# Layer 0 by feature tile: the modulation and the first projection of a hybrid denoising step

## The reference, cut to what matters

```python
def modulate(x, cond, g, w_mod, b_mod):
    mod = jax.nn.silu(cond) @ w_mod + b_mod          # (.., 3 * 1024): shift, scale, gate
    shift, scale, gate = jnp.split(mod[:, None, :], 3, axis=-1)
    return rmsnorm(x, g) * (1 + scale) + shift, gate

def project(x, cond, g, w_mod, b_mod, w_in):
    h, gate = modulate(x, cond, g, w_mod, b_mod)
    return split_proj(h @ w_in), gate
```

## Time and profile before

| | us |
|---|---|
| median of three runs | 1212.49 |
| the profiled execution, whole | 1213.18 |
| its span in the trace | 1211.2 |
| TensorE matmul busy | 1161.9 |
| VectorE busy | 612.7 |
| ScalarE busy | 442.5 |
| GpSimd busy | 364.7 |

### The profile page before, as it was taken

One profiled execution on the slowest core, in us unless ns is written; L12 is line 12 of the kernel. 1 busy time (PEld: TensorE's weight loads), 2 busy tenths in 40 slices (PEclk: granted clock), 3 DMA queues, 4 the chain that ended last, 5 costly groups with the idle time before them and its releaser, 6 DMA issues.

```text
span 1211.2 us, 20038 instructions
## 1 busy us (share of the span) xinstructions
PE 1161.9 (96%) x8022; PEld 1094.5 (90%) x8022; DVE 612.7 (51%) x1412; ACT 442.5 (37%) x1003; POOL 364.7 (30%) x284
## 2 busy tenths in 40 slices
PE   2699999999999999999999999999999999999996
PEld 0489989989989999999999999998999999999996
DVE  3567765765664542152385454676334451334256
ACT  3343535455443111152263344544444311124231
POOL 0123230245360221232362323114424212223342
PEclk9899999999999999999999999999999999999998
DMA  8503131232420112225461201132111011222334
GB/s 346 207 24 140 53 116 55 86 122 62 149 75 19 36 35 105 74 88 171 129 195 40 88 23 60 67 107 67 64 56 50 33 39 36 87 92 78 122 105 161
DMA packets 42860, 110.79 MB, mean 91 GB/s; under 512 B 6032, under 2 KB 21520, under 8 KB 41488
## 3 DMA queue, kind: packets, MB, share of 16 engines
q1 hardware_dynamic: 38736, 105.58, 25.6%
q10 hardware_dynamic: 4032, 3.93, 0.9%
HBM read 99.27 MB, written 10.22 MB: 90 GB/s over the span
## 4 chain that ended last, share of the span: by engine, by line
PE 84%; DVE 3%; issue 0%; ACT 0%; DVEq 0%; ACTq 0%
PE psum L986 67%; PE psum L1015 5%; PE psum L998 5%; PE psum L1006 4%; PE psum L1023 1%; PE psum L1032 1%; DVE xy L1281 1%; PE psum L1133 0%; DVE slots L1370 0%; PE psum L1041 0%; DVE slots L1576 0%; DVE slots L1367 0%; DVE prob L1450 0%; DVE slots L1374 0%; PE psum L188 0%
## 5 line engine op out<-in xcount | busy, mean ns | idle before, releaser
L986 PE MATMUL psum<-h_hi,w_hi 128*128 128x384 f32 x1728 | 604.9, 350 | 8.5 <-DVE h_lo L1253 8.4
L986 PE MATMUL psum<-h_hi,w_lo 128*128 128x384 f32 x1728 | 581.1, 336 | 0.0
L986 PE MATMUL psum<-h_lo,w_hi 128*128 128x384 f32 x1728 | 580.1, 336 | 0.0
L302 POOL TENSOR_TENSOR w_lo<-w_raw,w_hi 128x512 fp32r<-128x512 f32 x144 | 202.7, 1427 | 654.8 <-ACT w_hi L296 654.8
L986 PEld LDWEIGHTS psum<-h_hi,w_hi 128*128 128x128 f32 x1728 | 325.8, 189 | 30.5 <-issue 21.0
L986 PEld LDWEIGHTS psum<-h_lo,w_hi 128*128 128x128 f32 x1728 | 326.5, 189 | 0.0
L986 PEld LDWEIGHTS psum<-h_hi,w_lo 128*128 128x128 f32 x1728 | 325.6, 188 | 0.0
L296 ACT CAST w_hi<-w_raw 128x512 fp32r<-128x512 f32 x144 | 81.9, 618 | 173.2 <-PE psum L986 146.6
L875 ACT ACTIVATE prob<-prob,stat 128x512 f32<-128x512 f32 (+2 forms) x144 | 96.4, 671 | 91.5 <-DVE stat L1440 91.3
L1450 DVE TENSOR_SCALAR prob<-prob,stat 128x512 f32<-128x512 f32 (+1 forms) x144 | 83.4, 579 | 6.5
L882 ACT COPY prob<-psum 128x512 f32<-128x512 f32 (+1 forms) x144 | 75.2, 544 | 27.6 <-PE psum L1006 27.1
(11 more groups left out here) (108 smaller groups left out, 988.3 us busy)
## 6 DMA issues: line engine op xcount, KB each, us to landing
w_raw<-in_w_tiles SPq DMA_DIRECT2D x72, 512.0 KB, 3.3
xy<-in_w_mod SPq DMA_DIRECT2D x32, 512.0 KB, 4.3
table<-in_rpb SPq DMA_DIRECT2D x48, 192.0 KB, 3.5
slots<-in_w_mod SPq DMA_DIRECT2D x8, 1024.0 KB, 6.6
table<-in_w_tiles SPq DMA_DIRECT2D x16, 512.0 KB, 3.6
xy<-in_xT SPq DMA_DIRECT2D x8, 576.0 KB, 7.3
slots<-in_xT SPq DMA_DIRECT2D x8, 384.0 KB, 4.8
x_kept<-xy SPq DMA_DIRECT2D x8, 384.0 KB, 5.3
```

The source lines that it names most:

```text
L302: nc.gpsimd.tensor_tensor(w_lo[:, w % 2, a:b], RAW[raw_at(w)][:, a:b], w_hi[:, w % 2, a:b], ALU.subtract).then_inc(s.lo_ready, 1)
L986: last = nc.tensor.matmul(psum[:, bank, 0:CH], a[:, w % 2, k, :], h[:, k, cols], start=(k == order[0] and a is w_hi and h is h_hi), stop=( ...
```

## The change

The first block is gone; its work stands at the head of the second one, and each engine goes on without meeting the others. The modulation weights of layer 0 come in another layout: block k holds the shift and the scale columns of feature tile k for all 1024 inputs (again 1 MB). So each block finishes one feature tile. Tokens are projected feature tile by feature tile: for tile k the chunks 0 and 1 are one piece of 768 columns and chunk 2 (in two parts, latent and context) another, only tile 0 goes in three pieces; both output tiles and all three chunks accumulate at once in the six banks. The row of shifts and scales for tile k + 3 is made between the chunks of tile k.

```diff
@@ sync queue: four constants ahead of x instead of seven, masks last
+            for k in range(KT):
+                sp.dma_start(xy[:, k], xT[k]).then_inc(x_in[k], 16)
+            for k in range(KT):
+                if k >= 3:
+                    sp.wait_ge(wmod_used, k - 2)
+                sp.dma_start(wmod_sb[:, k % 3], w_mod0[k]).then_inc(wmod_in[k % 3], 16)
+                if k < 2:
+                    load_weights(sp, 0, k)
@@ ScalarE
+            def copy_row(k):
+                act.wait_ge(wmod_used, k + 1)
+                if k >= AHEAD:
+                    act.wait_ge(modT_ready, k - AHEAD + 1)
+                nc.scalar.copy(modrow[:, k % AHEAD], psum[:, ROW_BANK, 0:2 * P]).then_inc(modrow_ready, 1)
...
+            for k in range(KT):
+                act.wait_ge(x_in[k], 16)
+                if k > 2:
+                    act.wait_ge(squares_added, k - 2)
+                nc.scalar.activation(square_of(k) if k else squares, xy[:, k], ACT.Square).then_inc(x_squared, 1)
+            high_half(act, 0, 0)
+            copy_row(0)
+            high_half(act, 0, 1)
+            copy_row(1)
+            for c in range(NCH):
+                act.wait_ge(pro_norm[1], 3 * (c + 1))
+                nc.scalar.copy(first_rstd[:, cols_of(c)], psum[:, RSTD_BANK + c, 0:CH]).then_inc(pro_copied, 1)
+            copy_row(2)
+            for k in range(KT):
+                make_high(k)
+                if k + AHEAD < KT:
+                    copy_row(k + AHEAD)
@@ TensorE
+            def make_rows(k):
+                pe.wait_ge(wmod_in[k % 3], 16 * (k // 3 + 1))
+                if k >= 1:
+                    pe.wait_ge(modrow_ready, k)
+                for i in range(2):
+                    for q in range(4):
+                        last = nc.tensor.matmul(psum[32 * q:32 * q + 32, ROW_BANK, 0:2 * P], silu_c[:, 4 * i + q, :],
+                                                wmod_sb[:, k % 3, (4 * i + q) * 2 * P:(4 * i + q + 1) * 2 * P],
+                                                start=(i == 0), stop=(i == 1), skip_group_check=True)
+                last.then_inc(wmod_used, 1)
...
+            make_rows(0)
+            sums(0)
+            turn_row(0)
+            sums(1)
+            sums(2)
+            make_rows(1)
+            turn_row(1)
+            for c in range(NCH):
+                spread(c)
+            make_rows(2)
+            pe.wait_ge(pro_copied, NCH)
+            for k in range(KT):
+                project(k, 0)
+                if k + AHEAD < KT:
+                    make_rows(k + AHEAD)
+                project(k, 1)
+                if k + 2 < KT:
+                    turn_row(k + 2)
+                project(k, 2)
@@ VectorE: per tile the three modulation steps, then scaled and low by piece
+            for k in range(KT):
+                if k > 0:
+                    take_mods(k)
+                last = len(first_parts(k)) - 1
+                for i in range(last + 1):
+                    if k == 0:
+                        dve.wait_ge(pro_copied, i + 1)
+                    make_scaled(k, i)
+                    if i > 0:
+                        make_low(k, i - 1)
+                make_low(k, last)
+            settle()
```

More of the change, by code:

```diff
@@ new lines, in build, with first_parts @@
+        tanh_c = vectors[:, 272:272 + 2 * KT].rearrange("p (k c) -> p k c", c=2)
+        bmod_sb = vectors[:, 288:288 + 24 * DEPTH].rearrange("p (l n) -> p l n", l=DEPTH)
+        square_of = lambda k: slots[:, 10 if k % 2 else 7]
+        first_rstd = slots[:, 6]
+        first_scaled = (slots[:, 9], slots[:, 10])
+        AHEAD = 3
+        HALVES = ([(slice(0, 2 * CH), 0)], pieces(NCH - 1))
+        ROW_BANK, TURN_BANK, SUM_BANK = 6, 7, 0
+        def first_parts(k):
+            return [pieces(c) for c in range(NCH)] if k == 0 else HALVES
@@ new lines, in tensor_start, with turn_row, spread, project @@
+        def tensor_start(pe):
+            s = signals[0]
+            def make_rows(k):
[8 more added lines that the diff above has]
+                last.then_inc(wmod_used, 1)
+            def turn_row(k):
+                pe.wait_ge(modrow_ready, k + 1)
+                if k >= 1:
+                    pe.wait_ge(mod_taken, k)
+                for j in range(2):
+                    last = nc.tensor.transpose(psum[:, TURN_BANK, j * P:(j + 1) * P], modrow[:, k % AHEAD, j * P:(j + 1) * P],
+                                               ident[:, :])
+                last.then_inc(modT_ready, 1)
+            def spread(c):
+                for t in range(3 * c, 3 * c + 3):
+                    pe.wait_ge(pro_norm[0], t + 1)
+                    nc.tensor.matmul(psum[:, RSTD_BANK + c, (t % 3) * P:(t % 3 + 1) * P], ones[:, :], diag[:, t],
+                                     start=True, stop=True).then_inc(pro_norm[1], 1)
+            def project(k, c):
+                if c == 0 and k % 4 == 0:
+                    pe.wait_ge(s.lo_ready, k // 4 + 1)
+                if k == 0 or c != 1:
+                    pe.wait_ge(s.h_lo_ready, first_count(k, c if k == 0 else c // 2))
+                for n in range(2):
+                    if k % 4 == 0 and c == 0 and n == 1:
+                        pe.wait_ge(s.lo_ready, 2 + k // 4 + 1)
+                    for w, h in ((w_hi, h_hi), (w_hi, h_lo), (w_lo, h_hi)):
+                        last = nc.tensor.matmul(psum[:, 3 * n + c, 0:CH], w[:, n, k, :], h[:, k, cols_of(c)],
+                                                start=(k == 0 and w is w_hi and h is h_hi),
+                                                stop=(k == KT - 1 and w is w_lo), skip_group_check=True)
+                    if k == KT - 1:
+                        last.then_inc(s.chunk_done, 1)
+            def sums(c):
+                pe.wait_ge(squares_added, KT - 2 + c + 1)
+                for t in range(3 * c, 3 * c + 3):
+                    nc.tensor.matmul(psum[:, SUM_BANK, t:t + 1], squares[:, t * P:(t + 1) * P], ones[:, 0:1],
+                                     start=True, stop=True).then_inc(pro_sums, 1)
+            pe.wait_ge(cond_ready, 1)
+            pe.wait_ge(pro_ones, 1)
+            pe.wait_ge(consts_in, 16 * CONSTS)
+            make_rows(0)
[17 more added lines that the diff above has]
+                project(k, 2)
@@ L923, in y_high @@
                     nc.scalar.copy(h_hi[:, k, cols_of(c)], xy[:, k, cols_of(c)]).then_inc(s.y_hi_ready, 1)
[L925 to L931 removed]
+            if layer > 0:
                 for k in range(KT):
```

270 lines of the change are left out of this document (119 added, 151 removed).

## The result

The changed kernel takes 1208.85 us (median of six runs, 1205.76 to 1211.32), the kernel before 1213.37 (six runs). The ratio is 0.9967, interval 0.9953 to 0.9981: 4.5 us by the medians, 4.0 by the ratio. The forecast was 7.4. The six runs lie up to 5.6 us apart, the faster ones with the higher mean granted clock (see e8). The profiled execution of the changed kernel has a span of 1206.4 us against 1211.2.

The account below looks back on a forecast made before the run. TensorE is nearly always busy from 81 us, so tile 2's start decides: 32.4 + 6.8 + 4 x 4.95 + 2 x 4.25 + 3.2 = 70.7, with wait and clock 74.2 instead of 81.6; 1205.1 us, range 1199.5 to 1210.5.

Parts of the forecast that it names:

- the ring: Feature loop: projection, row, ScalarE's row copy, then next tile's high and low parts; 4.95 us per step, over TensorE's 4.65.
- the wait for tile 2: Behind the feature loop: TensorE waits about 2.6 us (2.3 to 3.8) for weight tile 2's low half.
- the transfer of the gain to the end: Behind tile 2: order, bytes and instructions stay as before, so the 7.4 us gain arrives at the end.
- (3), the first feature tile: Start, from block 0's rows through sums, root chain, diagonals and spreading: projection begins at 32.4 us.
- all slow: Start of projection with every term at its slow figure: 33.1 us.
- all fast: Start of projection with every term at its fast figure: 31.3 us.
- Step (4): Feature loop: first step 6.8 us, four middle steps 4.95 each, two last 4.25 each, last feature tile 3.2.
- Step (5): Handover to weight tile 2: its halves come late, TensorE waits about 2.6 us, tile 2 starts at 73.3.
- Step (6): Low clock behind the wait for tile 2: 3.4 us at half speed lose 1.7; half, 0.85, charged.
- The longer ring: Rival in the feature loop: a step takes 5.7 us, gain 4.4 or 2.3, middle 1209.1 us; chance 0.15.
- the end does not move: Rival behind tile 2: VectorE's backlog delays mixer C's scores at step 12, gain eaten, about 1212 us; chance 0.07.
- The rule weighed against the change: Feature loop: waits in every tile may bring half clock in every tile; as rival 1230, likely 1216.6 us, chance 0.08.

Follow-up runs that it names:

- e8: Changed kernel plus eight 128-column filling matmuls on TensorE behind the feature loop, in the wait for weight tile 2; 1208.16 us, ratio 0.9959 to the kernel before.
- e2: Changed kernel with GpSimd making the low half of weight tile 1 only after the first diagonal is written; 1208.12 us, ratio 0.9957 to the kernel before.
- e5: Changed kernel with GpSimd's low half of weight tile 1 waiting for the ninth diagonal; 1207.09 us, ratio 0.9954 to the kernel before.
- e6: Changed kernel with the edits of e3 and e5 together and more filling matmuls ahead of the second row's transposes; 1203.61 us, ratio 0.9923 to the kernel before.
- e9: Changed kernel with ScalarE's copy of row k + 3 behind the high part of tile k + 1; 1206.41 us, ratio 0.9947 to the kernel before.
- e4: Changed kernel with ScalarE's first high part ahead of the copy of row 2, that row made behind project(0, 0); 1210.37 us, ratio 0.9972.
- e1: Changed kernel run again without any edit; 1208.29 us, ratio 0.9956 to the kernel before.
- e3: Changed kernel plus 128-column filling matmuls, result unused, behind x squares and in three later waits before projection; 1205.15 us, ratio 0.9930 to the kernel before.
- e10: Changed kernel with ScalarE's casts of weight tile 2 ahead of the evacuation of chunk (0, 2) and its DMA issue; 1206.58 us, ratio 0.9945.

## Why the prediction was wrong

The direction held, and so did the mechanism behind the start of the projection: the feature loop, the ring, the wait for tile 2 and the transfer of the gain to the end were found where they were put, each right within 1 us. The gain was forecast at 7.4 and measured at 4.0 to 4.5.

**The step that failed is (3), the first feature tile,** as a sum: start 32.4, with 33.1 as its "all slow" end. It came at 37.16, outside its own bounds. Two terms were mis-sized and one was missing. Against the slow end, block 0 was 0.3 us late, from there to the root chain took 1.65 longer than forecast, the root chain 1.25, diagonals and spreading 1.5; the last part, from the rows of block 2 on, took 0.6 less, since the clock came back within those rows. That is the 4.1 us from 33.1 to 37.16.

- *Token sums and spreading at the low clock.* I took 2.14 and 2.69 us from the earlier trace rows as what small matmuls cost, and even called the second the slow figure. They had been run at the full level wholly or in part: the first in a stretch that the trace gives as full, and the second across its return. At the low level they cost 4.0 and 4.2; that is 1.9 and 1.5 us. Only the row matmuls had been priced at both levels. And I let the low level end at 30 us, where it ended before (29.8); it lasted to 34.7, and in none of the changed kernels without filling at the start did the clock come back ahead of 32.3.
- *GpSimd beside VectorE.* In the kernel before, no weight subtraction stood beside the root chain; in the change it does. I moved the weight tiles forward in the queue and asked only whether they were in time, and not what their GpSimd work would then stand beside. It cost 1.26 us in two instructions (0.41 and 1.19 instead of 0.17 each). e2 and e5 show it: with the subtractions elsewhere both took 0.17.
- *The choice between the ends.* With "all fast" at 31.3 and "all slow" at 33.1 the choice cost little. The fault was that the slow end was not the slow end.

e6 shows that the clock and GpSimd's place were nearly all of it: with both put right the start was 32.78, 0.4 from the forecast.

**Step (4), the loop,** was right in kind and 1 us too dear in each half: the first step took 5.8 (given were 5.4 for the full clock and 8.2 for the low one, taken 6.8), and a middle step 4.70 instead of 4.95. I had also written that TensorE's 4.65 would set the pace without the ring; e9 gave 4.56, and showed a value of the ring that no step of mine had, namely that the ring keeps VectorE from running ahead.

**Step (5)** was forecast at 2.6 and was 2.68. **Step (6)**, the low clock behind that wait, came in e4, e5 and e9 and not in the traces of the changed kernel, e1, e2, e3 or e6. Charging a half was fair, and its price, 1.7, was near the 1.6 measured; whether it comes is a matter of the execution, which no single trace decides.

**The rivals.** The longer ring gave 1209.1 us, next to the 1208.85 measured, but by a step of 5.7 that did not come: that agreement is chance. For "the end does not move" I had VectorE finish only 2 us before tile 2; it finished at 71.0, 5.5 us before, and the end moved.

**The rule weighed against the change**, the Trainium skill's (TensorE: Matmul & The Clock Gate, HAM oscillation) that a loop with a wait in every tile can fall to the half clock in every tile, did not show: from 37.1 to 73.8 us the clock was full. It was a mild case: TensorE waited 0.6 to 1.0 us in three of the seven steps and under 0.2 in the others. In e4, e5 and e10 the clock was low in the first step, behind the wait for the first high and low part. The clock did most of its harm ahead of the loop.

## What to carry to other kernels

A duration of a small matmul belongs to the clock level at which it ran; before it goes into a sum for another place, find out that level from a repeated instruction of known cost, and price both levels for every term. When work is moved forward, ask of each engine that it involves what it will now run beside, not only whether it is in time. A copy that stands ahead of the bottleneck's supplier in an in-order queue can cost more than the waits seen beside it, since it takes away the lead that the supplier could have gained: here 0.5 us in the four steps with the copy and 1.2 in the two behind them (e9).

## What the runs showed of the hardware

- The low level at the start of the program does not show in the granted clock of the kernels without filling: the column says 1.00 until the first record (34.7 us in the changed kernel), and the same eight row matmuls take 1.94 us there and 1.07 with the filling ahead of them.
- A nine-column VectorE instruction of 0.17 us took 1.19 us beside a GpSimd subtraction (two of them 1.20 each in e3), and nine diagonals 3.92 instead of 1.85. Each instruction held up ended within 0.1 us of the end of a subtraction. One that read PSUM and started at 25.81, inside the first subtraction, took its 0.17 us.
- After a busy loop of 36 us, one and the same wait of 2.7 us was followed by 3.4 us of the low level in three traces (e4, e5, e9) and by none in five (the changed kernel, e1, e2, e3, e6).
- The wait of 0.71 us and the 1.5 us of one-column matmuls in the norm at about 590 us were followed by 3.4 us of the low level in eight traces of fourteen. Such a stretch cost about 1.6 us of the time.
